# Gated linear attention inside a two-block layer: chunks of 128 tokens in place of 64, decays measured from the middle of a chunk, masks as bits, and the two directions' scores added by GpSimd

## The chip, the core and the metric

One core of a Trainium2 chip runs one program, which holds the two blocks of a layer. Times are device microseconds (us) of that core, as the median of several runs; lower is better. The engines are TensorE (PE; its weight loads are listed apart as PEld), VectorE (DVE), ScalarE (ACT), GpSimd (POOL) and SyncE (SP), which issues most of the transfers.

## The reference

The first block (attention, a gated delta rule, a gated mix) is not touched. The second block normalises its input, mixes tokens with a gated linear attention in both directions plus an average pooling, and ends with a mixture of 32 experts. The part that matters is the linear attention over 512 tokens, with 4 heads of 64 key and 128 value features, and with start states that a scan over 256 context tokens gives:

```
b = cumsum(la, within a chunk)                   # la: log of the decay, <= 0
k_st = k * exp(b_last - b)
d_state = k_st^T v                               # one 64x128 matrix a chunk and head
S_next = exp(b_last) * S + d_state               # scan over the chunks
qb, kb = q * exp(b), k * exp(-b)
scores = where(mask, qb kb^T, 0)
o = scores v + qb S_prev
out = o_f + flip(o_b)                            # both directions added
```

The reference uses CHUNK = 64. Its result does not depend on the chunk length but for rounding.

## The kernel before

Everything stays in one large SBUF tile, `arena`, whose parts are handed on from stage to stage. Every engine runs one list of instructions, written by hand, and waits on named semaphores. `bank("s")` and `bank("v")` give TensorE the next of four PSUM banks of two rings, `pss` (read by ScalarE, mostly) and `psv` (read by VectorE, mostly). `L.did` makes an engine wait for its own instruction; `L.need` waits for another engine's.

The linear attention lies at 1071 to 1142 us of the trace, in three parts.

1. Decays (1071 to 1092 us). For the four pairs of direction `d` and pair of heads `m2`, `decay_sums` sums the log decays of each tile of 128 tokens by a product with a triangle of ones that is cut at 64 tokens (`blk`). ScalarE makes `eb`, `enb` (exp of plus and minus the sum) and `dec2` (exp at the chunk's last token); VectorE multiplies them into `qb` and `kb` (`decayed`). `decay_rests` gives the sums from a token to its chunk's end; ScalarE and VectorE turn them into the keys `kst`. The pooling's products (`pool`) lie between.
2. Scan (1092 to 1117 us). Twelve steps `n`: four chunks of the context, then eight of the sequence. A step issues `kst^T v` of 64 tokens for both directions (line 1401); VectorE adds them to the decayed state (line 3174) and keeps the state ahead of each sequence chunk in `sprev`. In steps 0, 2, 4 and 6 lie the scores of one pair (line 1412), which VectorE multiplies with the mask (lines 3186, recorded as the helper's line 2621). Other products are put between: `pool_out` (line 1352), `gate_row` (line 1377), and, ahead of step 9, a product with the router's weights (recorded as L884), whose result ScalarE copies to `lshift`.
3. Outputs (1117 to 1142 us). For each `m2` two banks collect `scm v` of both directions (line 1426, 32 products of 128 columns in all) and `sprev^T qb` per chunk (line 1430, 64 products of 64 columns, with the two heads in the two halves of the array's rows).

After that ScalarE squares and copies the four results (lines 2271, 2272), TensorE sums the squares (line 1457), and the output projection and the router follow. The weights of the output projection's last part, `wo23`, are loaded into the place where `sprev` lay, so SyncE issues that load (line 1670) when the outputs' products are done, and line 1457 waits for it. Behind it SyncE issues the first loads of the experts' weights.

## Time and profile before

| | |
|---|---|
| median of 3 runs | 1481.84 us (1479.63 to 1483.26) |
| the profiled execution | 1489.19 us, of which the profile's span is 1487.4 us |
| TensorE busy | 1400.6 us, 94% of the span |
| VectorE busy | 723.8 us, 49% |
| ScalarE busy | 382.0 us, 26% |
| GpSimd busy | 421.5 us, 28% |
| mean granted clock of TensorE | 0.972 of full speed |

Busy shares are means over stages with different limits; what counts for the change is which wait ends last in the linear attention's own 70 us.

### The profile page before, as it was taken

The page shows a single profiled execution, that of the slowest core. Times are in us where ns is not written, and L with a number is a line of the kernel's source. Part 1 is how long each engine was busy: PE and PEld are TensorE (multiplying, and loading weights), DVE is VectorE, ACT ScalarE, POOL GpSimd, SP SyncE. Part 2 cuts the span into 40 slices and gives each one's busy share as a digit, 9 for nine tenths or more (in the row PEclk, how much of TensorE's full clock was granted, in tenths as well). Part 3 has the DMA queues.
Part 4 walks back from the last instruction along what each step waited for, and adds up shares of the span by engine and source line. Part 5 has one row for each costly group of instructions (what it writes and reads, how often), then busy time and mean ns, then how long its engine had stood idle before and what let it go on. Part 6 is the DMA issues. An engine that isn't in the chain of part 4 may idle for free. (4 is left out here: it accounts for less than half of the span.)

```text
span 1487.4 us, 22182 instructions
## 1 busy us (share of the span) xinstructions
PE 1400.6 (94%) x8580; PEld 966.8 (65%) x8580; DVE 723.8 (49%) x1284; ACT 382.0 (26%) x773; POOL 421.5 (28%) x316
## 2 busy tenths in 40 slices
PE   6998999999999989999999999999998979998876
PEld 4865556885554458778888868878867864333222
DVE  5261572124449988778624252731471454332325
ACT  2313564104343233332110022511531011000002
POOL 3410020620005526654545535045000003111110
PEclk9999999999999999999999999999996988999999
DMA  8227210113112113314232311241302858999996
GB/s 318 88 86 285 83 58 29 71 71 113 57 58 85 57 58 147 141 59 187 111 134 96 142 57 57 65 124 57 121 26 108 345 207 309 416 419 419 422 417 258
DMA packets 48439, 236.51 MB, mean 159 GB/s; under 512 B 12135, under 2 KB 13423, under 8 KB 27600
## 3 DMA queue, kind: packets, MB, share of 16 engines
q1 hardware_dynamic: 42720, 224.48, 38.8%
q0 software_dynamic: 5040, 8.27, 1.5%
q10 hardware_dynamic: 576, 2.36, 0.4%
q8 instruction: 69, 1.13, 0.3%
q14 instruction: 34, 0.28, 0.1%
HBM read 223.66 MB, written 21.51 MB: 165 GB/s over the span
## 5 line engine op out<-in xcount | busy, mean ns | idle before, releaser
L922 PE MATMUL psv<-arena 128*128 128x256 f32 x1648 | 362.8, 380 | 1.9 <-DVE arena L2691 1.9
L922 PEld LDWEIGHTS psv<-arena 128*128 128x128 f32 x1648 | 314.1, 191 | 46.0 <-issue 3.2
L2624 DVE TENSOR_TENSOR arena<-arena,psv 128x512 f32<-128x512 f32 (+1 forms) x99 | 68.6, 693 | 275.4 <-PE psv L922 273.4
L884 PE MATMUL psv<-arena,wslot 128*128 128x512 f32 x384 | 170.7, 598 | 0.0
L1542 PE MATMUL pss<-arena 128*64 128x512 f32 x432 | 122.2, 636 | 14.7 <-DMA arena<-w_expert_in 13.6
L884 PEld LDWEIGHTS psv<-arena,wslot 128*128 128x128 f32 x384 | 71.2, 190 | 83.2 <-issue 82.9
L884 PE MATMUL pss<-arena 128*128 128x512 f32 (+1 forms) x256 | 106.2, 568 | 1.4 <-ACT arena L2019 1.4
L2854 DVE SCALAR_TENSOR_TENSOR arena<-psv,ccols,arena 128x510 f32<-128x510 f32 (+1 forms) x96 | 71.9, 749 | 50.0 <-ACT arena L2075 46.7
L922 PE MATMUL psv<-arena,wslot 128*128 128x256 f32 x384 | 86.3, 380 | 2.3 <-DVE arena L2624 1.3
L1885 ACT ACTIVATE arena<-pss 128x512 f32<-128x512 f32 (+2 forms) x89 | 51.5, 579 | 129.0 <-PE pss L884 64.3
L1542 PEld LDWEIGHTS pss<-arena 128*64 128x64 f32 x432 | 38.3, 145 | 69.8 <-issue 69.7
L884 PEld LDWEIGHTS pss<-arena 128*128 128x128 f32 x256 | 47.7, 190 | 51.6 <-issue 48.4
L922 PEld LDWEIGHTS psv<-arena,wslot 128*128 128x128 f32 x384 | 72.6, 190 | 13.2 <-issue 2.3
L922 PE MATMUL psv<-wslot,arena 128*128 128x256 f32 x320 | 72.6, 381 | 6.2 <-ACT arena L1944 2.7
L2408 POOL TENSOR_TENSOR arena<-wslot 128x1024 f32<-128x1024 f32 x11 | 26.4, 2396 | 176.5 <-PE pss L1064 90.4
L2426 POOL TENSOR_TENSOR arena<-arena 128x1024 f32<-128x1024 f32 x20 | 49.1, 2453 | 81.0 <-DVE arena L2717 35.8
L922 PEld LDWEIGHTS psv<-wslot,arena 128*128 128x128 f32 x320 | 60.3, 190 | 16.0 <-ACT arena L1944 3.9
L3328 DVE TENSOR_TENSOR arena<-pss,arena 128x256 f32<-128x256 f32 x16 | 6.8, 425 | 128.7 <-ACTq L233 128.7
L2621 DVE TENSOR_TENSOR arena<-arena 128x512 f32<-128x512 f32 (+2 forms) x64 | 51.4, 803 | 32.6 <-ACT arena L2031 22.3
L1561 PE MATMUL psv<-arena 128*64 128x512 f32 x236 | 54.8, 598 | 3.0 <-ACTq L233 1.6
L2624 DVE TENSOR_TENSOR arena<-arena 128x512 f32<-128x512 f32 (+4 forms) x67 | 53.4, 797 | 3.0
L2295 ACT ACTIVATE arena<-pss 128x256 f32<-128x256 f32 x16 | 6.2, 384 | 184.0 <-PE pss L1542 184.0
(411 smaller groups left out, 2066.7 us busy)
## 6 DMA issues: line engine op xcount, KB each, us to landing
wslot<-w_blocks SPq DMA_DIRECT2D x56, 1024.0 KB, 5.2
arena<-w_blocks SPq DMA_DIRECT2D x30, 1024.0 KB, 6.3
arena<-w_expert_out SPq DMA_DIRECT2D x29, 1024.0 KB, 25.0
arena<-w_expert_in SPq DMA_DIRECT2D x28, 1024.0 KB, 26.7
arena<-w_expert_in SPq DMA_DIRECT2D x28, 512.0 KB, 7.9
arena<-w_expert_in SPq DMA_DIRECT2D x6, 2048.0 KB, 25.7
y_dram<-arow SPq DMA_DIRECT2D x1, 4096.0 KB
arena<-c_pool SPq DMA_DIRECT2D x4, 1024.0 KB, 8.8
```

What stands on the lines that cost most here:

```text
L884: m = mm(o, l, r, start=(n == 0), stop=(n == len(pairs) - 1))
L922: m = mm(o[:, j * HALF_T:(j + 1) * HALF_T], l[:, c, j * P:(j + 1) * P], r[:, c, :], start=new and j == 0 and c == 0, stop=j == 1 and c == ...
L1542: m = mm(o[x * CAP:(x + 1) * CAP, :], xe[:, k, c, x * CAP:(x + 1) * CAP], win[2 * w + x][:, c, :], start=(c == 0), stop=(c == KC - 1))
L1561: m = mm(o[x * CAP:(x + 1) * CAP, :], hidT[:, k, c, x * CAP:(x + 1) * CAP], wout_home(n, x, c)[:, c0:c0 + 512], start=(c == 0), stop=(c == 1))
L1885: L.did(A(dst, src, func, **kw), s[sig] if sig else None, [s["free_s"]])
L2295: L.did(A(sil[:, k, :], pss[:, (q0 + job) % 4, 0:DE], ACT.Silu), None, [s["sil_ready"]])
L2408: L.did(TT(part[0], a21, a22, ALU.add), s["part_ready"])
L2426: L.did(TT(term[n], lo, hi, ALU.subtract), s["term_ready"])
L2621: L.did(V.tensor_tensor(o, x, y, ALU.mult), *sig)
L2624: L.did(V.tensor_tensor(o, x, y, ALU.add), *sig)
L2854: L.did(V.scalar_tensor_tensor(o[:, lo:hi], b[:, lo + m:hi + m], tap(j, k), o[:, lo:hi], ALU.mult, ALU.add), s["conv_ready"] if k == 4 els ...
L3328: L.did(V.tensor_tensor(hid[:, k, :], pss[:, (s0 + job) % 4, DE:2 * DE], sil[:, k, :], ALU.mult), s["hid_ready"], [s["free_s"], s["sil_use ...
```

## The change

Chunks are 128 tokens, one tile, so the scan has two context steps and three sequence steps whose state is needed on (`LAST_STATE` = 5), and each step contracts 128 tokens.

The sums that go into `eb` and `enb` are now taken from the middle of the tile: the constants `sums_of` hold the triangle less the column of the first (or last) half, and two further columns that give the tile's whole sum and the sum up to its middle. So the product has 130 columns for a sequence tile and 2 for a context tile, and `dec2` holds both decays. A state is needed as seen from the middle too: ScalarE multiplies each `sprev` by the decay up to the middle, 16 instructions of 128x128 into the half of `sprev` that is now free.

The scores of a pair lie in each of the steps 0 to 3. Their mask is no product with 0 or 1 any more, but a bitwise AND of the scores' bits with a mask of integers, `kept`, that VectorE makes once (two instructions). GpSimd adds the scores of the two directions, four instructions of 128x512, so line 1426's products are half as many.

```diff
@@ -82,10 +85,14 @@
-    c[:, C_BLE:C_BLE + P] = same & (p <= f)
-    c[:, C_BGE:C_BGE + P] = same & (p >= f)
-    c[:, C_BGT:C_BGT + P] = same & (p > f)
-    c[:, C_BLT:C_BLT + P] = same & (p < f)
+    c[:, C_BLE:C_BLE + P] = p <= f
+    c[:, C_BGE:C_BGE + P] = p >= f
+    c[:, C_BGT:C_BGT + P] = p > f
+    for d, (sums, half) in enumerate(((p <= f, p < CH2), (p >= f, p >= CH2))):
+        o = C_SUMS + d * GSUM
+        c[:, o:o + P] = sums.astype(np.float32) - half
+        c[:, o + P:o + P + 1] = 1.0
+        c[:, o + P + 1:o + P + 2] = half
...
@@ -279,8 +286,10 @@
-        blk = [const[:, C_BLE:C_BLE + P], const[:, C_BGE:C_BGE + P]]
-        blk_rest = [const[:, C_BGT:C_BGT + P], const[:, C_BLT:C_BLT + P]]
+        kept_both = ctx.enter_context(nc.sbuf_tensor("kept", [P, 2, P], I32))
+        kept = [kept_both[:, d, :] for d in range(2)]
+        sums_of = [const[:, C_SUMS + d * GSUM:C_SUMS + (d + 1) * GSUM] for d in range(2)]
+        rest_of = [const[:, C_BGT:C_BGT + P], const[:, C_LT:C_LT + P]]
...
@@ -792,25 +801,20 @@
             r = P // GRID_W
             return max(0, r * t - below) * GRID_W, min(SEQ // GRID_W, r * t + r + above) * GRID_W
-        def chunk_at(d, n):
-            c = n if n < 4 else n - 4
-            if d:
-                c = (3 if n < 4 else 7) - c
-            return (NT if n < 4 else 0) + c // 2, c % 2
-        def chunk_col(d, n):
-            t, u = chunk_at(d, n)
-            return 2 * t + u
+        def tile_at(d, n):
+            if n < NTC:
+                return NT + (NTC - 1 - n if d else n)
+            return NT + NTC - 1 - n if d else n - NTC
         def state_at(d, m2, n):
-            if n < 4:
+            if n < NTC:
                 return swork[:, n % 2, d, m2, :]
-            if n == 12:
-                return None
-            t, u = chunk_at(d, n)
-            return sprev[:, d, m2, 2 * t + u, :]
+            return sprev[:, d, m2, tile_at(d, n), :]
+        LAST_STATE = NT + NTC - 1
+        DELTA_STATES = 4 * (NCK - 1)
         def scale_rows(eng, L, V, g):
@@ -1324,16 +1328,19 @@
             def decay_sums(n):
                 d, m2 = divmod(n, 2)
                 col = d * 256 + m2 * P
-                for t0, many in ((0, NT), (NT, NTC)):
-                    o = bank("s")
-                    for t in range(many):
-                        m = mm(o[:, t * P:(t + 1) * P], la[:, t0 + t, col:col + P], blk[d], start=True, stop=True)
+                for tiles in (range(NT - 1), range(NT - 1, NT + NTC)):
+                    o, at_ = bank("s"), 0
+                    for t in tiles:
+                        r = sums_of[d] if t < NT else sums_of[d][:, P:]
+                        n_ = GSUM if t < NT else 2
+                        m = mm(o[:, at_:at_ + n_], la[:, t, col:col + P], r, start=True, stop=True)
+                        at_ += n_
                     m.then_inc(s["full_s"], 1)
             def decay_rests(t):
                 o = bank("s")
                 for d in range(2):
-                    m = mm(o[:, d * 256:(d + 1) * 256], blk_rest[d], la[:, t, d * 256:(d + 1) * 256],
+                    m = mm(o[:, d * 256:(d + 1) * 256], rest_of[d], la[:, t, d * 256:(d + 1) * 256],
                            start=True, stop=True)
                 m.then_inc(s["full_s"], 1)
@@ -1379,31 +1386,29 @@
                 m.then_inc(s["full_s"], 1)
             L.need(s["k2_ready"])
-            for n in range(12):
-                if n in (0, 4, 6):
+            for n in range(LAST_STATE):
+                if n in (0, 2, 3):
                     L.need(s["kst_ready"], 2)
-                for g in {0: (0, 1), 1: (2,), 2: (3,)}.get(n, ()):
+                for g in {0: (0, 1), 1: (2, 3)}.get(n, ()):
                     pool_out(g)
-                if n in (3, 5):
-                    gate_row(0 if n == 3 else 4)
-                if n == 9:
+                if n in (2, 3):
+                    gate_row(0 if n == 2 else 4)
+                if n == 4:
                     pe.wait_ge(s["ld_wrt"], 32)
                     o = bank("s")
                     product(o[:, 0:NG + NE], [(mod[:, 24 + c, 0:1].broadcast_to([P, P]), wrt[:, c, :])
                                               for c in range(KC)]).then_inc(s["full_s"], 1)
                 for d in range(2):
-                    t, u = chunk_at(d, n)
+                    t = tile_at(d, n)
                     o = bank("v")
-                    tok = slice(u * CH2, (u + 1) * CH2)
                     for m2 in range(2):
                         for hh in range(2):
                             h = 2 * m2 + hh
-                            m = mm(o[HX[hh], m2 * P:(m2 + 1) * P], kst[tok, t, d * 256 + h * 64:d * 256 + (h + 1) * 64],
-                                   v2[tok, t, h * P:(h + 1) * P], start=True, stop=True)
+                            m = mm(o[HX[hh], m2 * P:(m2 + 1) * P], kst[:, t, d * 256 + h * 64:d * 256 + (h + 1) * 64],
+                                   v2[:, t, h * P:(h + 1) * P], start=True, stop=True)
                     m.then_inc(s["full_v"], 1)
-                if n % 2 == 0 and n < 2 * H2:
-                    m2, d = divmod(n // 2, 2)
+                if n < 2 * 2:
+                    m2, d = divmod(n, 2)
                     if n == 0:
                         L.need(s["qb_ready"], 4)
                     o = [bank("v"), bank("v")]
@@ -1414,21 +1419,22 @@
                     for hh in range(2):
                         m[hh].then_inc(s["full_v"], 1)
-            L.need(s["sc_ready"], 2 * H2)
-            L.need(s["sprev_ready"])
             for m2 in range(2):
+                L.need(s["scm_ready"], 2)
                 o = [bank("s"), bank("s")]
+                for hh in range(2):
+                    h = 2 * m2 + hh
+                    for t in range(NT):
+                        tk = slice(t * P, (t + 1) * P)
+                        mm(o[hh][:, tk], v2[:, t, h * P:(h + 1) * P], scm[2 * h][:, tk],
+                           start=t == 0, stop=False, skip_group_check=True)
+                if m2 == 0:
+                    L.need(s["sprev_ready"], 2 * 2 * NT)
                 for d in range(2):
-                    for hh in range(2):
-                        h = 2 * m2 + hh
-                        for t in range(NT):
-                            tk = slice(t * P, (t + 1) * P)
-                            mm(o[hh][:, tk], v2[:, t, h * P:(h + 1) * P], scm[2 * h + d][:, tk],
-                               start=(d == 0 and t == 0), stop=False, skip_group_check=True)
-                    for c in range(8):
-                        ck = slice(c * CH2, (c + 1) * CH2)
-                        m = [mm(o[hh][:, ck], sprev[HX[hh], d, m2, c, :], qb[HX[hh], d, m2, ck], start=False,
-                                stop=(d == 1 and c == 7), skip_group_check=True) for hh in range(2)]
+                    for t in range(NT):
+                        tk = slice(t * P, (t + 1) * P)
+                        m = [mm(o[hh][:, tk], sprev[HX[hh], d, m2, NT + t, :], qb[HX[hh], d, m2, tk], start=False,
+                                stop=(d == 1 and t == NT - 1), skip_group_check=True) for hh in range(2)]
                 for hh in range(2):
                     m[hh].then_inc(s["full_s"], 1)
             products_by["attention", 0] = jobs["s"]
@@ -2249,13 +2255,19 @@
                 b = full()
                 if n >= 2:
                     act.wait_ge(s["qb_ready"], n - 1)
-                L.did(A(eb[:, n % 2, :], b, ACT.Exp, scale=1.0 / GATE_NORM))
-                L.did(A(enb[:, n % 2, :], b, ACT.Exp, scale=-1.0 / GATE_NORM))
-                ends = b.rearrange("p (c i) -> p c i", i=CH2)[:, :, CH2 - 1 if d == 0 else 0]
-                L.did(A(dec2[:, d, m2, 0:8], ends, ACT.Exp, scale=1.0 / GATE_NORM), s["bexp_ready"], [s["free_s"]])
+                b = b[:, 0:(NT - 1) * GSUM].rearrange("p (t i) -> p t i", i=GSUM)
+                most = slice(0, (NT - 1) * P)
+                L.did(A(eb[:, n % 2, most].rearrange("p (t i) -> p t i", i=P), b[:, :, 0:P], ACT.Exp,
+                        scale=1.0 / GATE_NORM))
+                L.did(A(enb[:, n % 2, most].rearrange("p (t i) -> p t i", i=P), b[:, :, 0:P], ACT.Exp,
+                        scale=-1.0 / GATE_NORM))
+                L.did(A(dec2[:, d, m2, 0:NT - 1, :], b[:, :, P:GSUM], ACT.Exp, scale=1.0 / GATE_NORM), s["bexp_ready"],
+                      [s["free_s"]])
                 b = full()
-                ends = b[:, 0:CTX].rearrange("p (c i) -> p c i", i=CH2)[:, :, CH2 - 1 if d == 0 else 0]
-                L.did(A(dec2[:, d, m2, 8:12], ends, ACT.Exp, scale=1.0 / GATE_NORM), s["bexp_ready"], [s["free_s"]])
+                L.did(A(eb[:, n % 2, (NT - 1) * P:], b[:, 0:P], ACT.Exp, scale=1.0 / GATE_NORM))
+                L.did(A(enb[:, n % 2, (NT - 1) * P:], b[:, 0:P], ACT.Exp, scale=-1.0 / GATE_NORM))
+                L.did(A(dec2[:, d, m2, NT - 1:, :].rearrange("p t k -> p (t k)"), b[:, P:P + 2 * (1 + NTC)], ACT.Exp,
+                        scale=1.0 / GATE_NORM), s["bexp_ready"], [s["free_s"]])
             for t in STATES:
                 evict(kst[:, t, :], 512, "kexp_ready", ACT.Exp, scale=1.0 / GATE_NORM)
             L.did(A(ss[:, 60:61], eps, ACT.Sqrt))
@@ -2265,6 +2277,13 @@
             for c0 in (0, 512):
                 evict(gtrow[:, c0:c0 + 512], 512, None)
             evict(lshift, NG + NE, None)
+            for n in range(NTC, NT + NTC):
+                for d in range(2):
+                    t = tile_at(d, n)
+                    act.wait_ge(s["st_ready"], DELTA_STATES + 2 * (n - NTC) + d + 1)
+                    for m2 in range(2):
+                        L.did(A(sprev[:, d, m2, NT + t, :], sprev[:, d, m2, t, :], ACT.Copy,
+                                scale=dec2[:, d, m2, t, 1:2]), s["sprev_ready"])
             L.need(s["qb_ready"], 4)
             for h in range(H2):
                 b = full()
@@ -2519,6 +2538,10 @@
+            for m2 in range(2):
+                L.need(s["sc_ready"], 4)
+                for h in (2 * m2, 2 * m2 + 1):
+                    L.did(TT(scm[2 * h], scm[2 * h], scm[2 * h + 1], ALU.add), s["scm_ready"])
...
@@ -3149,6 +3172,8 @@
+            for d, c in enumerate((C_BLE, C_BGE)):
+                L.did(V.tensor_scalar(kept[d], const[:, c:c + P], -1.0, None, ALU.mult))
...
@@ -3164,27 +3189,21 @@
             pooled(3)
             L.did(V.memset(swork[:, 0, :, :, :], 0.0))
-            for n in range(12):
+            assert L.raised[s["st_ready"]] == DELTA_STATES, L.raised[s["st_ready"]]
+            for n in range(LAST_STATE):
                 for d in range(2):
                     b = full()
-                    c = chunk_col(d, n)
-                    if n == 11:
-                        L.raise_(s["free_v"])
-                        continue
-                    ins = [V.scalar_tensor_tensor(state_at(d, m2, n + 1), state_at(d, m2, n), dec2[:, d, m2, c:c + 1],
+                    t = tile_at(d, n)
+                    ins = [V.scalar_tensor_tensor(state_at(d, m2, n + 1), state_at(d, m2, n), dec2[:, d, m2, t, 0:1],
                                                   b[:, m2 * P:(m2 + 1) * P], ALU.mult, ALU.add) for m2 in range(2)]
                     L.go(ins[0])
-                    if d:
-                        L.did(ins[1], s["free_v"])
-                    else:
-                        L.go(ins[1], s["free_v"])
-                if n % 2 == 0 and n < 2 * H2:
-                    m2, d = divmod(n // 2, 2)
+                    L.did(ins[1], s["st_ready"] if n + 1 >= NTC else None, [s["free_v"]])
+                if n < 2 * 2:
+                    m2, d = divmod(n, 2)
                     for hh in range(2):
                         b = full()
-                        mul(by4(scm[2 * (2 * m2 + hh) + d]), by4(b), over(blk[d], 4), s["sc_ready"], [s["free_v"]])
-            L.raise_(s["sprev_ready"])
+                        L.did(V.tensor_tensor(by4(scm[2 * (2 * m2 + hh) + d].bitcast(I32)), by4(b.bitcast(I32)),
+                                              over(kept[d], 4), ALU.bitwise_and), s["sc_ready"], [s["free_v"]])
             for h in range(H2):
                 L.need(s["rt2_ready"])
                 o = catT[:, h, :]
```

Two places show how the instructions stand now. TensorE, from the last score products through the scan's end and the outputs (`pss` and `psv` are the two rings of banks, `wrt` the router's weights). Before:

```order
L1401 MATMUL psv<-arena 64x128 x16
L1412 MATMUL psv<-arena 128x128 x8
L1401 MATMUL psv<-arena 64x128 x16
L884 MATMUL pss<-wrt,mod 128x36 x8
L1401 MATMUL psv<-arena 64x128 x24
L1426 MATMUL pss<-arena 128x128 x8
L1430 MATMUL pss<-arena 128x64 x16
```

And now, where L1384 is `gate_row`, L1407 the scan's product, L1417 the scores, L888 the router's product, L1429 and L1436 the outputs:

```order
L1384 MATMUL pss<-const,mod 128x128 x4
L1407 MATMUL psv<-arena 64x128 x8
L1417 MATMUL psv<-arena 128x128 x8
L888 MATMUL pss<-wrt,mod 128x36 x8
L1407 MATMUL psv<-arena 64x128 x8
L1429 MATMUL pss<-arena 128x128 x8
L1436 MATMUL pss<-arena 128x128 x16
L1429 MATMUL pss<-arena 128x128 x8
L1436 MATMUL pss<-arena 128x128 x16
```

Behind the router's product stand 8 products of the scan instead of 24, and the outputs are 48 products, all of 128 columns, instead of 96.

ScalarE, from the pooling's results to the outputs' squares. Before (L2264 scales the pooling's results, L1885 copies `gtrow` and then `lshift`, L2271 and L2272 square and copy a head's output):

```order
L2264 ACTIVATE arena<-pss,cols 128x512 x4
L1885 ACTIVATE gtrow<-pss 128x512 x2
L1885 ACTIVATE arena<-pss 128x36
L2271 ACTIVATE arena<-pss 128x512
L2272 ACTIVATE arena<-pss 128x512
```

And now:

```order
L2276 ACTIVATE arena<-pss,cols 128x512 x4
L1891 ACTIVATE gtrow<-pss 128x512 x2
L1891 ACTIVATE arena<-pss 128x36
L2285 ACTIVATE arena<-arena 128x128 x16
L2290 ACTIVATE arena<-pss 128x512
L2291 ACTIVATE arena<-pss 128x512
```

All 16 scalings of the states (L2285) stand behind the copy of `lshift`, which waits for the router's product.

## Rows read from the trace of the kernel before

**Rows 1.** The page: granted clock of TensorE in 40 slices of 37 us, tenths.

```profile
PEclk9999999999999999999999999999996988999999
```

**Rows 2.** Windows: length, busy of PE, PEld, DVE, ACT, POOL, then clock, DMA share, GB/s.

```profile
1094.00:1117.00 23.00, 21.08 (x293) 16.32 (x292) 18.02 (x53) 3.68 (x7) 0.00 (x0) 0.91 0.00 1
1117.00:1142.00 25.00, 24.75 (x192) 23.55 (x192) 1.50 (x2) 2.40 (x5) 0.00 (x0) 0.61 0.00 1
1142.00:1147.00 5.00, 0.01 (x1) 0.04 (x3) 1.50 (x2) 2.38 (x4) 0.00 (x0) 0.65 0.81 308
```

**Rows 3.** Windows again, shorter ones around the clock's changes, and one of the experts.

```profile
1105.00:1112.00 7.00, 5.90 (x95) 4.79 (x94) 6.12 (x17) 0.60 (x1) 0.00 (x0) 1.00 0.00 0
...
1117.00:1130.00 13.00, 12.79 (x82) 12.26 (x82) 0.00 (x0) 0.00 (x0) 0.00 (x0) 0.50 0.00 0
1130.00:1136.00 6.00, 6.00 (x38) 5.66 (x38) 1.50 (x2) 2.39 (x4) 0.00 (x0) 0.50 0.01 3
1137.00:1142.00 5.00, 4.96 (x68) 4.64 (x66) 0.00 (x0) 0.01 (x1) 0.00 (x0) 1.00 0.00 0
...
1300.00:1400.00 100.00, 86.89 (x398) 33.13 (x396) 31.81 (x77) 5.38 (x14) 17.02 (x29) 0.95 1.02 420
```

**Rows 4.** Timeline of PE in the scan; two records are one product.

```profile
1092.40 1.88 PE L1352 MATMUL pss<-arena 128*128 128x512 f32 x4
1094.21 0.68 PE L1401 MATMUL psv<-arena 64*64 64x128 f32 x16
1094.82 1.16 PE L1412 MATMUL psv<-arena 64*128 64x128 f32 x16
...
1100.34 1.16 PE L1377 MATMUL pss<-const,mod 128*128 128x128 f32 x8
...
1111.16 2.21 PE L884 MATMUL pss<-wrt,mod 128*128 128x36 f32 x16
1113.30 3.53 PE L1401 MATMUL psv<-arena 64*64 64x128 f32 x48
```

**Rows 5.** Timeline of PE in the outputs and at the stage behind them.

```profile
1120.89 3.68 PE L1430 MATMUL pss<-arena 64*128 64x64 f32 x32
1124.50 3.78 PE L1426 MATMUL pss<-arena 128*128 128x128 f32 x16
...
1137.98 2.05 PE L1426 MATMUL pss<-arena 128*128 128x128 f32 x16
1139.96 2.00 PE L1430 MATMUL pss<-arena 64*128 64x64 f32 x32
1146.99 1.94 PE L1457 MATMUL pss<-arena,const 128*32 128x512 f32 x8 [5.03 <-DMA arena<-w_blocks]
```

**Rows 6.** Timeline of SP's queue at the outputs' end.

```profile
1142.03 0.34 SPq L1670 DMA_DIRECT2D arena<-w_blocks  x1
```

**Rows 7.** Timelines of ACT and PE in the decays.

```profile
1081.08 0.60 ACT L2252 ACTIVATE arena<-pss 128x512 f32<-128x512 f32 x1 [0.55 <-DVE arena L2621]
...
1082.95 2.77 ACT L1885 ACTIVATE arena<-pss 128x512 f32<-128x512 f32 x4
...
1082.62 1.99 PE L1336 MATMUL pss<-arena,const 128*128 128x256 f32 x8 [0.29 <-ACTq L233]
```

**Rows 8.** Timeline of DVE at the end of the decays and in the scan.

```profile
1092.67 0.69 DVE L3145 COPY arena<-psv 128x512 f32<-128x512 f32 x1 [2.11 <-PE psv L1345]
...
1094.99 1.12 DVE L3174 SCALAR_TENSOR_TENSOR arena<-arena,psv 128x128 f32<-128x128 f32 x4 [0.86 <-PE psv L1401]
1096.15 1.53 DVE L2621 TENSOR_TENSOR arena<-psv,const 128x512 f32<-128x512 f32 x2
```

**Rows 9.** Timeline of PE elsewhere: products of the form 128x64 by 128 columns.

```profile
523.82 1.09 PE L968 MATMUL pss<-const,arena 128*64 128x128 f32 x16
```

**Rows 10.** Groups by form, whole trace: busy, mean ns | idle before.

```profile
L1971 ACT ACTIVATE arena<-arena 128x128 f32<-128x128 f32 x40 | 11.9, 297 | 21.2 <-DVE arena L2624 21.1
...
L1914 ACT ACTIVATE arena<-pss,gain 128x128 f32<-128x128 f32 x16 | 5.9, 368 | 25.1 <-PE pss L960 24.7
...
L2384 POOL TENSOR_TENSOR arena<-arena 128x512 f32<-128x512 f32 x16 | 18.5, 1158 | 7.9 <-ACTq L1920 5.4 <-ACT arena L1885 1.6
```

More of the change, by code:

```diff
@@ L10 @@
 U32 = mybir.dt.uint32
+I32 = mybir.dt.int32
 ALU = mybir.AluOpType
@@ L56 @@
 C_BLE = C_DG + CK
-C_BGE, C_BGT, C_BLT = C_BLE + P, C_BLE + 2 * P, C_BLE + 3 * P
-C_IOTA = C_BLE + 4 * P
+C_BGE, C_BGT = C_BLE + P, C_BLE + 2 * P
+C_SUMS = C_BLE + 3 * P
+GSUM = P + 2
+C_IOTA = C_SUMS + 2 * GSUM
 C_TOK = C_IOTA + CAP
@@ L457, in build @@
         enb = at(top[0], 2, SEQ)
-        dec2 = at(top[0], 2, 2, 12)
+        dec2 = at(top[0], 2, 2, NT + NTC, 2)
         swork = at(top[0], 2, 2, 2, P)
```

2 lines of the change are left out of this document (1 added, 1 removed).

## The prediction

> **What bounds the kernel now.** I looked first for where TensorE loses time. The page's row of granted clocks has one dent in the middle of the run, in two slices around 1120 us [rows 1], and the linear attention lies there. Its windows show two stretches. In the scan (1094 to 1117 us) TensorE is busy 21.1 of 23 us and VectorE 18.0, in short pieces that wait for one another. In the outputs (1117 to 1142 us) TensorE is busy 24.75 of 25 us, nobody else has work, and its mean clock is 0.61 [rows 2]. The shorter windows say why 0.61: the clock is full up to 1112 us, at half (1.2 of 2.4 GHz) from 1117 to 1136 us though the engine is never idle, and full again from 1137 us [rows 3]. So eight products of 128 columns take 3.78 us at half clock and 2.05 at full, and sixteen of 64 columns 3.68 and 2.00 [rows 5]. TensorE sets the end of this stage, mostly at half clock.
>
> What hangs on that end? SyncE issues the load of `wo23` at 1142.03 us, as the outputs end [rows 6], and TensorE sits 5.03 us until it has landed [rows 5]. The transfer engines move nothing before it: 0.00 of their time in the scan and in the outputs [rows 2]. The experts' weights come behind this load on the same queue, at 420 GB/s with a DMA share of 1.02 later on [rows 3]. A stage bound by transfers would swallow a gain only if its transfers were already under way; here they start after the outputs. If the outputs end X earlier, the load, the projection, the router and the experts all start X earlier. So the working is that of one moment: the outputs' end, 1141.96 us now (1139.96 plus 2.00) [rows 5].
>
> **The change, step by step, at full clock unless said.**
>
> *Decays.* ScalarE has six instructions a pair instead of four: two of 384 columns, two of 128 and two tiny ones, for two of 512 and two tiny. A pair takes 1.87 us now (1081.08 to 1082.95) [rows 7]; the two of 384 save some 0.2, the two of 128 cost about 0.3 each [rows 10], so about 0.4 more. That is 1.6 us on ScalarE for four pairs, part of it in time in which it waits for VectorE. TensorE's `decay_rests` wait for the banks that ScalarE frees (0.29 us now) [rows 7], so I add 0.45 us to TensorE's path. VectorE comes about 1 us later, hidden by its 2.11 us of waiting for the last pooling product [rows 8]; without that cover it would be 1 us. `decay_sums` has as many products as before, narrow ones among them; I cost it at nothing, and the cover is the same wait. The two instructions that make `kept` fall into a pause of VectorE earlier on. The scan starts at 1092.40 + 0.45 = 1092.85 us [rows 4].
>
> *Scan.* Twelve pairs of 64-token products become five of 128 tokens. A pair costs 0.61 us now (1094.21 to 1094.82) [rows 4]. The new form, 128x64 weights and 128 columns with two heads side by side, occurs elsewhere: eight products in 1.09 us [rows 9], about 1.05 without the last one's drain. So 5 x 1.05 = 5.25. The rest stays: four `pool_out` 3.6 (two take 1.8, 1092.40 to 1094.21), four scores 4 x 1.1, two `gate_row` 2 x 1.1, the router's product 2.2 [rows 4]. Sum 17.65, so the router's product ends at 1109.45 us and the last scan product at 1110.5. VectorE is no bound: a step is four updates (1.12) and two masks (1.53) [rows 8], 2.8 us with the gaps, while TensorE needs 3.25 and more for each of steps 1 to 3. This takes the AND for as fast as the product that it replaces; no row has it, and the bounds are the 1.53 us of two products and, above, the rival below. The first half of the score-by-`v` products, now eight, needs GpSimd's sums of the first two heads. Their masks are done at about 1102.6, and GpSimd's sum of this size takes 1.16 us [rows 10], so they are there at about 1105, and those of the other two heads at about 1112. Both are early: hidden by the scan, and worth 2.3 us in the worst case if that were gone. The eight products add 2.0 us: 1112.5 us.
>
> *A new wait.* Next TensorE needs all 16 scaled states, and these stand on ScalarE behind the copy of `lshift`, hence behind the router's product. They could begin with the first sequence state; they begin at 1109.75 us. One costs between 0.30 us (SBUF to SBUF, no scale taken from memory) and 0.37 (from PSUM, with such a scale) [rows 10]. Both properties meet here, and each waits for its predecessor, so I take 0.42 a piece with the gap, bounds 0.33 and 0.45: 6.7 us, until 1116.5. TensorE sits 4.0 us, and queued behind are all the remaining outputs, for which ScalarE's squares and the load wait. So by this point most of what the shorter scan gave is used up: 1116.5 against the 1117.2 at which the outputs began (1113.30 plus 3.53, and a short pause) [rows 4], but with the first eight products already done.
>
> *Outputs.* Left are 16 state products, 8 of scores, 16 of states. State products with 128 columns have the form of the scores (eight in 1.1 us at full clock) [rows 4]: 2.2 a group, and 2.0 for the eight of 128 rows. At full clock 6.4 us, end 1122.9. At half clock the eight take 3.75, and sixteen state products between 3.68 (their old form of half the columns) and 4.4 (twice 2.2) [rows 5]; with 4.2 that is 12.1 us, end 1128.6. The clock: before, it fell in the scan, and the pause of 4 us is a second occasion, as it is low in the pause from 1142 to 1147, too (mean 0.65) [rows 2]. But the products of 64 columns, under which it stayed low for 19 us, are gone, and it came back during a group of the dense ones. The rows do not decide between the ends, so I take the middle, 1125.7 us.
>
> The sum: 1141.96 - 1125.7 = 16.3 us. Against it, the constants have 132 columns more, 67 KB, 0.2 us at the 420 GB/s of [rows 3] if the start waits for all of it. Net 16.1 us. The profiled execution took 1489.19 us (span 1487.4), 7.3 us above the median of the runs, so it would become 1473.1, and the median 1481.84 - 16.1 = 1465.7 us.
>
> **A page against the trace.** The rows show TensorE busy without a break from 1117 to 1136 us at 0.50 of its clock [rows 3]. The Trainium skill (TensorE: Matmul & The Clock Gate, "What's actually happening") says that the throttled clock is the default and that the engine's activity releases it. By that rule the dense outputs would run at full clock nearly from their start, and the sum would be 19 us in place of 16; the trace agrees only in part, since 19 us of unbroken work did not release it.
>
> **The rivals.**
>
> *Full clock in the outputs.* The work after the pause is all of the dense kind that brought the clock back. End at 1122.9, gain 18.9, time 1462.9 us. Against it: the pause just ahead.
>
> *Half clock to the end.* The clock stays low over the whole 12.1 us, as it did over 19. End at 1128.6, gain 13.2, time 1468.6 us.
>
> *A dearer wait.* ScalarE's copies cost 0.6 us each (a form not in the trace, and a semaphore to wait for each time): 9.6 us, until 1119.4, 2.9 us later than in my sum, and with the low clock behind it the end is at 1131, gain 10 to 11, time about 1471 us.
>
> *The experts swallow it.* If the transfers of the experts' weights were bound by something that does not move with the outputs, the time would stay at 1481.8. For it: a DMA share of 1.02 in that stage [rows 3]. Against it: no transfer runs before 1142 us [rows 2].
>
> *Slower.* VectorE's AND on 32-bit integers out of PSUM is slow. The trace has no such row; the product that it replaces takes 0.76 us. To eat the 16 us and VectorE's spare time in the scan (about 0.5 us in each of four steps), eight of them would have to cost 18 us more, 2.3 each; from 3.1 us an AND on, the kernel is slower. With 4 us an AND it would be 8 x 3.3 - 2 - 16, about 8 us slower: 1490 us. I see no reason for it.
>
> **How the numbers follow.** A measurement here tells about 0.3%, 4.4 us, from no change. Chances: my forecast, a clock that is mixed (1463.5 to 1468), 0.45; full clock 0.15; half clock 0.17; dearer wait or another loss in part 0.12; swallowed 0.07; slower 0.04. Faster: the first four, 0.89; same 0.07; slower 0.04. The range holds the first three and most of the fourth: from 1460 (full clock, and copies at 0.33 us) to 1473 (dearer wait and half clock). The predicted time is 1465.7 us.
>
> **What the profile would show.** Right: the AND at about 0.7 us; the router's product ending near 1109.5; the copies of the states starting only behind `lshift` and ending near 1116.5, with TensorE idle for about 4 us until then; the outputs ending between 1123 and 1129; and from `wo23`'s load on the same rows, 16 us earlier. Wrong: a DVE wait between scores and scan products; states that are ready before TensorE asks; GpSimd's sums asked for before they are there; or a distance from the load of `wo23` to the end that is not that of before. The prediction is most exposed to TensorE's clock, in the outputs and in the first products behind the load, and to the price of ScalarE's copies.

## The result, and the profile after

The changed kernel takes 1473.97 us (median of five, 1471.97 to 1475.90) where the kernel before takes 1481.84 (1479.63 to 1483.27) on the same chip. The ratio is 0.9941 with an interval of 0.9923 to 0.9959: 7.9 us or 0.59% faster. I had predicted 1465.7 us, with a range up to 1473. The sign is right and the size is half of what I said (16.1 us).

The profiled execution of the changed kernel took 1475.9 us (span 1473.9). First its page: busy times, then TensorE's granted clock in 40 slices of 37 us, to be held against [rows 1].

```profile
PE 1387.6 (94%) x8372; PEld 952.7 (65%) x8372; DVE 717.0 (49%) x1262; ACT 389.6 (26%) x797; POOL 426.2 (29%) x320
...
PEclk9999999999999999999999999999998989999989
```

The slice of the dent (the 31st, 1115 to 1153 us before) is an 8 now and was a 6. (It is one slice, not two, as I had it; the two 8s behind it in [rows 1] lie at 1190 to 1264 us, behind the linear attention.) The timeline of PE in the scan and the outputs, which answers to [rows 4, 5]:

```profile
1095.03 1.88 PE L1359 MATMUL pss<-arena 128*128 128x512 f32 x4
1096.84 1.09 PE L1407 MATMUL psv<-arena 128*64 128x128 f32 x16
1097.87 1.16 PE L1417 MATMUL psv<-arena 64*128 64x128 f32 x16
...
1109.39 1.97 PE L888 MATMUL pss<-wrt,mod 128*128 128x36 f32 x16
1111.30 1.09 PE L1407 MATMUL psv<-arena 128*64 128x128 f32 x16
1112.32 2.05 PE L1429 MATMUL pss<-arena 128*128 128x128 f32 x16
1118.69 3.55 PE L1436 MATMUL pss<-arena 64*128 64x128 f32 x32 [4.32 <-ACT arena L2285]
1122.17 2.15 PE L1429 MATMUL pss<-arena 128*128 128x128 f32 x16
1124.25 2.06 PE L1436 MATMUL pss<-arena 64*128 64x128 f32 x32
1131.42 1.94 PE L1463 MATMUL pss<-arena,const 128*32 128x512 f32 x8 [5.11 <-DMA arena<-w_blocks]
```

The windows of the same kernel (length, busy of PE, PEld, DVE, ACT, POOL, clock, DMA share, GB/s):

```profile
1096.00:1118.00 22.00, 18.37 (x199) 14.56 (x197) 12.08 (x29) 9.96 (x22) 5.08 (x4) 1.00 0.00 1
1118.00:1127.00 9.00, 7.61 (x80) 7.08 (x80) 1.50 (x2) 3.63 (x8) 0.00 (x0) 0.81 0.01 2
```

The predicted wait stands where it was predicted: TensorE waits 4.32 us for ScalarE's L2285, the copies of the scaled states. Ahead of it the clock is full, through the whole scan. Behind it the granted clock is at half (0.50) from 1119 to 1122 us, so the first group of state products takes 3.55 us where the last one, at full clock, takes 2.06; the next group is nearly all at full clock (2.15 us for 2.05). Now the other engines. ACT and POOL by their timelines, then two groups of the lines by form:

```profile
1111.41 0.20 ACT L1891 ACTIVATE arena<-pss 128x36 f32<-128x36 f32 x1 [3.42 <-PE pss L888]
1111.73 6.91 ACT L2285 ACTIVATE arena<-arena 128x128 f32<-128x128 f32 x16
```
```profile
1104.70 2.62 POOL L2544 TENSOR_TENSOR arena<-arena 128x512 f32<-128x512 f32 x2 [61.66 <-DVE arena L3205]
1111.17 2.62 POOL L2544 TENSOR_TENSOR arena<-arena 128x512 f32<-128x512 f32 x2 [3.85 <-DVE arena L3205]
```
```profile
L2285 ACT ACTIVATE arena<-arena 128x128 f32<-128x128 f32 x16 | 6.4, 401 | 0.6
...
L3205 DVE TENSOR_TENSOR arena<-psv,kept 128x512 int32<-128x512 int32 x8 | 5.5, 692 | 1.2 <-PE psv L1417 0.5
```

The sixteen copies run one straight after the other behind the router's copy, 6.91 us in all, 0.43 us each. The bitwise mask costs 0.69 us. GpSimd's sums are ready at 1107.3 and 1113.8 us, before TensorE asks for them (1112.3 and 1122.2). SyncE issues the load of `wo23` again as the outputs end (1126.31 us), where it stood at 1142.03 us in [rows 6]:

```profile
1126.37 0.34 SPq L1676 DMA_DIRECT2D arena<-w_blocks  x1
```

**Where the difference to the profile of before comes from.** I mark one stretch in each trace: L, from the first `pool_out` product (the start of the scan) to the end of the outputs. Before it was 1092.40 to 1141.96, 49.56 us; after it is 1095.03 to 1126.31, 31.28 us. My prediction had 1092.85 to 1125.7, 32.85 us. So this stretch became 18.3 us shorter where I said 16.7 (16.3 net of the 0.45 us ahead of it). The spans, though, differ by 13.5 us only (1487.4 to 1473.9): the rest of the program is 4.8 us longer (1442.6 for 1437.8): 2.6 us ahead of the marked stretch (1095.03 for 1092.40), of which 0.45 were predicted, and 2.2 behind it. And the medians differ by 7.9 us. So the mechanism is all there, and yet half the gain is missing against the median. Two theories:

A. The stretch of low clock in the outputs of before has no fixed length. The profiled execution of before, 7.3 us above its median, had a long one; a typical execution has a shorter one, and there is less to gain than I took from it.

B. The gain is the same in every execution, and some 8 us of it are lost elsewhere: in the experts, or in the start with its larger constants.

If A holds, L of before varies, and the rest does not differ between the two kernels. If B holds, the rest is longer in the changed kernel.

### The profile page after: what moved, and what is told of

It is laid out like the page before. It is cut to its first block, busy times and chain, and to the rows that moved or that the text cites. A ratio compares the mean times of both kernels' runs of the same rounds, so it can differ in the third digit from the quotient of the medians.

```text
span 1473.9 us, 21769 instructions
## 1 busy us (share of the span) xinstructions
PE 1387.6 (94%) x8372; PEld 952.7 (65%) x8372; DVE 717.0 (49%) x1262; ACT 389.6 (26%) x797; POOL 426.2 (29%) x320
## 4 chain that ended last, share of the span: by engine, by line
PE 77%; DVE 10%; DMA 5%; SPq 3%; ACT 2%; issue 2%; DVEq 0%; POOL 0%; ACTq 0%; POOLq 0%
PE psv L926 33%; PE psv L888 14%; PE pss L888 7%; PE pss L1548 5%; DMA arena<-w_expert_in 4%; PE psv L1567 2%; DVE arena L2647 2%; SPq L1694 2%; PE pss L1068 1%; DVE arena L2967 1%; PE pss L972 1%; PE pss L989 1%; DVE arena L2644 1%; DVE arena L2932 1%; PE psv L964 1%
## 5 line engine op out<-in xcount | busy, mean ns | idle before, releaser
L888 PE MATMUL psv<-arena,wslot 128*128 128x512 f32 x384 | 170.7, 598 | 0.0
L888 PEld LDWEIGHTS psv<-arena,wslot 128*128 128x128 f32 x384 | 71.2, 190 | 83.2 <-issue 82.9
L888 PE MATMUL pss<-arena 128*128 128x512 f32 (+1 forms) x256 | 106.2, 568 | 1.4 <-ACT arena L2025 1.4
L926 PE MATMUL psv<-wslot,arena 128*128 128x256 f32 x320 | 75.6, 392 | 6.2 <-ACT arena L1950 2.7
L888 PEld LDWEIGHTS pss<-arena 128*128 128x128 f32 x256 | 47.7, 190 | 51.6 <-issue 48.4
```

Of the source, the lines that this page charges most:

```text
L888: m = mm(o, l, r, start=(n == 0), stop=(n == len(pairs) - 1))
L926: m = mm(o[:, j * HALF_T:(j + 1) * HALF_T], l[:, c, j * P:(j + 1) * P], r[:, c, :], start=new and j == 0 and c == 0, stop=j == 1 and c == ...
```

## The experiments

Below, "its chip's before" is the kernel before as timed beside the run on the same chip. Ratios are to it, with 95% intervals. before_a, before_b, after_a and early ran on one chip, the other runs on another.

**The kernel before, thrice more (before_a, before_b, before_c), and the changed one again (after_a).** No edit.

> The kernel before, unchanged, profiled once more. My prediction took the outputs' 24.8 us and the clock of 0.61 in them from one profiled execution of 1489.2 us, 7.3 us above the median. Theory A (the profiled execution is not typical: the clock stays low in the outputs for a length that differs from one execution to the next): a median near 1482, and in this profile the outputs take another time than 24.8 us, from about 14 (full clock) to 25 us, with the whole time moving by the same amount. Theory B (the local gain is the 16 to 18 us that the two profiles show in every execution, and the changed kernel loses 8 us elsewhere): the outputs take 24 to 25 us again, and this execution too lies near 1482 to 1489 us.

> The kernel before a further time, one look. By theory A the outputs' length differs from the other two profiles of this kernel, anywhere from 14 to 25 us; by theory B it is 24 to 25 us for the third time.

> The changed kernel, unchanged, profiled once more, on the same chip as the kernel before. Both theories: 0.994 of the kernel before, 8 us. Theory A: the stretch from the first output product to the last (13.99 us in the first profile, of which 4.3 us a wait for the states) differs by up to 4 us by the clock. Theory B: the stages outside the linear attention are 5 to 8 us longer than those of the kernel before in both profiles.

> One more look at the kernel before. Its outputs have taken 24.8, 17.3 and 21.4 us in three profiles, with the clock low for 23.8, 9 and 20 us from its fall on. If the length of the low stretch differs freely from one execution to the next, this look gives a fourth value between 16 and 25 us; most executions (1477 to 1482 us of span) should look like the shortest.

Times: before_a 1484.32 us, ratio 1.0015 (0.9989 to 1.0041); after_a 1472.08, ratio 0.9928 (0.9901 to 0.9955). That is a gain of 9.8 us against its chip's before (1481.88) and of 12.2 against before_a, the same kernel on the same chip. The profile of before_a (span 1480.3), timeline of PE in the outputs and one window:

```profile
1118.32 3.65 PE L1426 MATMUL pss<-arena 128*128 128x128 f32 x16 [0.37 <-issue]
1121.89 2.00 PE L1430 MATMUL pss<-arena 64*128 64x64 f32 x32
...
1133.63 2.00 PE L1430 MATMUL pss<-arena 64*128 64x64 f32 x32
1140.66 1.93 PE L1457 MATMUL pss<-arena,const 128*32 128x512 f32 x8 [5.03 <-DMA arena<-w_blocks]
```
```profile
1118.00:1136.00 18.00, 17.32 (x192) 16.52 (x192) 1.50 (x2) 2.72 (x5) 0.00 (x0) 0.90 0.00 1
```

The same instructions in the same order, but only the first group of the outputs is slow; the clock is back at 1122 us, where it came back between 1136 and 1137 us before [rows 3]. In before_b (span 1490.4) it came back during the fourth group:

```profile
1119.88 3.75 PE L1426 MATMUL pss<-arena 128*128 128x128 f32 x16 [0.38 <-issue]
...
1130.89 2.58 PE L1430 MATMUL pss<-arena 64*128 64x64 f32 x32
```

and in before_c (span 1488.9) during the sixth, as in the first profile:

```profile
1117.35 3.75 PE L1426 MATMUL pss<-arena 128*128 128x128 f32 x16 [0.38 <-issue]
...
1135.67 2.54 PE L1430 MATMUL pss<-arena 64*128 64x64 f32 x32
1138.14 2.05 PE L1426 MATMUL pss<-arena 128*128 128x128 f32 x16
```

Put side by side, with L and the rest of the span (microseconds):

| profile | span | L | rest |
|---|---|---|---|
| before, the one predicted from | 1487.4 | 49.6 | 1437.8 |
| before_a | 1480.3 | 41.7 | 1438.6 |
| before_b | 1490.4 | 46.4 | 1444.0 |
| before_c | 1488.9 | 49.6 | 1439.3 |
| after | 1473.9 | 31.3 | 1442.6 |
| after_a | 1470.3 | 31.2 | 1439.1 |

L of before spreads over 8 us, and that of the changed kernel does not move, though up to 4 us of movement had been allowed for it. The rest is 1438 to 1444 us, and its spread is common to both kernels: its mean is 1439.5 us over the six profiles of this study with a scan of 64 tokens, and 1440.1 over the seven with 128 tokens. So B's 5 to 8 us are not there. That speaks for A and against B. The unprofiled executions say which length is typical: in most of each chip's before, the span is 1477 to 1483 us with a mean clock of 0.975 to 0.979, as in before_a; in some (4 of 18 on this chip, 7 of 25 on the other one) it is 1484 to 1494 us. That 41.7 us is the typical L rests on this span and on one profile. With it the gain in L is 10.4 to 10.5 us, less 0.5 for the longer decays ahead of it, and the runs show 7.9 to 12.2 by medians (the interval of the first, 0.9923 to 0.9959, is itself 6 to 11 us). One expectation missed: before_c was to look like the typical ones most likely, and showed the long stretch again. Three of the four profiles had a stretch longer than the typical; why profiled executions should, or whether three of four is chance, stays open.

**ScalarE's copies as soon as their states are there (early).** The same instructions; only the place of the copies in ScalarE's program changes.

```diff
-            for c0 in (0, 512):
-                evict(gtrow[:, c0:c0 + 512], 512, None)
-            evict(lshift, NG + NE, None)
-            for n in range(NTC, NT + NTC):
+            def middle_states(n):
...
+            evict(gtrow[:, 0:512], 512, None)
+            middle_states(NTC)
+            evict(gtrow[:, 512:1024], 512, None)
+            middle_states(NTC + 1)
+            middle_states(NTC + 2)
+            evict(lshift, NG + NE, None)
+            middle_states(NTC + 3)
```

> ScalarE scales the states of the first three sequence steps between its other copies, ahead of the router's product, and only the last step's four behind it. If the wait of 4.3 us is owed to their place in ScalarE's list, the last state is ready 0.5 to 1 us after TensorE asks, so 3.5 us are saved, and up to 3 us more if the pause was what kept the clock low behind it: 0.2 to 0.45% faster than the changed kernel, 1467.5 to 1470.5 us. If the wait was only a part of a bound that something else sets (VectorE's last update), TensorE waits for that and nothing is saved.

1465.05 us (1463.71 to 1468.71), ratio 0.9885 (0.9851 to 0.9919), against 0.9928 of the changed kernel beside it: 7.0 us less. It is also faster than expected (1467.5 to 1470.5 us), because no wait at all is left where 0.5 to 1 us was expected. ACT and PE of its timeline:

```profile
1105.41 3.44 ACT L2282 ACTIVATE arena<-arena 128x128 f32<-128x128 f32 x8
1108.89 0.20 ACT L1891 ACTIVATE arena<-pss 128x36 f32<-128x36 f32 x1
1109.62 1.70 ACT L2282 ACTIVATE arena<-arena 128x128 f32<-128x128 f32 x4 [0.53 <-DVE arena L3202]
```
```profile
1109.30 2.05 PE L1429 MATMUL pss<-arena 128*128 128x128 f32 x16
1111.37 2.06 PE L1436 MATMUL pss<-arena 64*128 64x128 f32 x32
1113.36 2.05 PE L1429 MATMUL pss<-arena 128*128 128x128 f32 x16
1115.34 2.06 PE L1436 MATMUL pss<-arena 64*128 64x128 f32 x32
1122.44 1.88 PE L1463 MATMUL pss<-arena,const 128*32 128x512 f32 x8 [5.05 <-DMA arena<-w_blocks]
```

The wait is gone, and the low clock with it. L is 25.40 us for 31.18. Of these 5.8 us, 4.3 are the wait and 1.5 the clock (3.55 less 2.06). The last microsecond of the 7.0 is within the intervals. Taken once more (early_b, below), this version took 1467.59 us, with the same L and the clock full again. It beats both kernels.

**Both groups of score products ahead of the wait (swap).** TensorE works on while ScalarE copies.

```diff
+            both = []
             for m2 in range(2):
                 L.need(s["scm_ready"], 2)
                 o = [bank("s"), bank("s")]
+                both.append(o)
...
-                if m2 == 0:
-                    L.need(s["sprev_ready"], 2 * 2 * NT)
+            L.need(s["sprev_ready"], 2 * 2 * NT)
+            for m2 in range(2):
+                o = both[m2]
```

> The changed kernel with TensorE's second group of score products ahead of its wait for the scaled states, where the first stands; ScalarE's order is not touched. The group takes 2.0 us and falls into the wait, which shrinks from 4.3 to 2.3 us: 2 us faster than the changed kernel. If the low clock of the first state products (3.55 us for what takes 2.06) comes from the pause, a pause of 2.3 us makes it rarer, up to 1.5 us more: 1468.5 to 1470.5 us. If only ScalarE's order mattered, no change.

1469.99 us (1467.92 to 1472.58), ratio 0.9908 (0.9878 to 0.9939). Timeline of PE, and a window over the state products:

```profile
1110.59 3.84 PE L1431 MATMUL pss<-arena 128*128 128x128 f32 x32
1116.96 5.27 PE L1439 MATMUL pss<-arena 64*128 64x128 f32 x64 [2.53 <-ACT arena L2288]
```
```profile
1116.90:1122.30 5.40, 5.27 (x64) 5.08 (x64) 0.48 (x1) 1.60 (x4) 0.00 (x0) 0.71 0.01 3
```

The wait shrinks by 1.8 us, the length of the second group, to 2.53, and L to 28.9. The clock (mean 0.71) is low behind the shorter pause too, for a part of 5.27 us where full clock takes 4.1. So what is left of the wait costs about 3.7 us (2.5 of waiting and 1.2 of clock), as the step to early (another 3.5 in L) confirms.

**The sums of both directions undone in the changed kernel (no_add), the same in early (early_no_add), and done alone in the kernel before (before_add).** The score products go back to one set for each direction, or, in the kernel before, become one set with GpSimd's sums ahead. The edit of no_add; that of before_add is its reverse:

```diff
-                L.need(s["scm_ready"], 2)
+                L.need(s["sc_ready"], 4)
...
+                for d in range(2):
...
-                        mm(o[hh][:, tk], v2[:, t, h * P:(h + 1) * P], scm[2 * h][:, tk],
-                           start=t == 0, stop=False, skip_group_check=True)
+                            mm(o[hh][:, tk], v2[:, t, h * P:(h + 1) * P], scm[2 * h + d][:, tk],
+                               start=(d == 0 and t == 0), stop=False, skip_group_check=True)
...
-            for m2 in range(2):
-                L.need(s["sc_ready"], 4)
-                for h in (2 * m2, 2 * m2 + 1):
-                    L.did(TT(scm[2 * h], scm[2 * h], scm[2 * h + 1], ALU.add), s["scm_ready"])
```

> The changed kernel without GpSimd's sums: TensorE runs all 32 score products again, everything else as changed. Two groups of eight come back, 2.0 us each at full clock. The first falls into the wait of 4.3 us for the scaled states and should cost nothing; the second lies on the path. So 2 us slower than the changed kernel (1474 to 1476 us) if the wait is a wait as read, 4 us slower if it is not. With the pause down to 2.3 us the clock may stay up, which would give 1 to 2 us back.

> The kernel before with one part of the change: GpSimd adds the two directions' scores and TensorE runs 16 score products instead of 32; chunks of 64 tokens, masks by product, everything else as before. The products left out cost 2.0 us for eight at full clock. If the part is worth what its products cost, the outputs become 4.0 us shorter at equal clock (16 at full clock becomes 12) and the run about 0.27% faster. If the outputs were set by the clock rather than by the work, less dense work keeps the clock low for longer and part of the 4 us is lost: 0 to 0.15%.

no_add: 1475.01 us (1471.18 to 1481.61), ratio 0.9949 (0.9929 to 0.9969), 1 to 3 us above the changed kernel's two medians, neither of which was timed beside it. L is 31.48, 0.2 to 0.3 more than with the sums, though TensorE has 3.6 us more of products to do. Timeline of PE:

```profile
1111.39 3.84 PE L1430 MATMUL pss<-arena 128*128 128x128 f32 x32
1117.77 2.06 PE L1437 MATMUL pss<-arena 64*128 64x128 f32 x32 [2.53 <-ACT arena L2286]
1119.75 3.84 PE L1430 MATMUL pss<-arena 128*128 128x128 f32 x32
```

Eight products of the sixteen lie in the wait (2.53 for 4.32), and here the clock came out full behind it, which saves 1.5 us: 3.6 - 1.8 in the wait - 1.5 is the 0.3 of L. So in the changed kernel GpSimd's sums gained little in L; by the medians, whose intervals overlap, 1 to 3 us. before_add: 1478.55 us (1473.42 to 1484.56), ratio 0.9965 (0.9940 to 0.9989), 3.7 us less than its chip's before (1482.29), where the sixteen products left out are worth 4.0 at full clock.

> The kernel with the scaled states moved ahead in ScalarE's list, once more. Its first profile showed no pause at all and full clock in the outputs (8.1 us from first to last product). If both belong together, the second profile shows the same, and the median lies at 1464 to 1467 us. If the clock was luck, this profile has a low stretch in the outputs and the executions spread like those of the changed kernel.

> The same without GpSimd's sums: TensorE runs all 32 score products. In the changed kernel leaving the sums out cost 1 to 3 us only, as the first group's 2.0 us fell into the wait for the states. If that wait is why the sums give less than their 4 us, they give the whole 4 us here, where there is no wait: outputs of 12 us at full clock in place of 8.1, and 1468.5 to 1470.5 us. If the sums are worth less for another reason (GpSimd takes 1.31 us each, VectorE's updates are 0.06 us longer in the changed kernel), it is again 1 to 3 us.

early_b 1467.59 us, ratio 0.9897 (0.9868 to 0.9925); early_no_add 1472.28, ratio 0.9927 (0.9899 to 0.9954). Both lie above the times expected of them (by 0.6 and 1.8 us); the difference is near the 4 us expected. Between them lie 4.7 us of medians and 3.5 us of L (25.39 and 28.88). With the wait gone the sums are worth what their two groups of eight products take, 1.79 us each, 3.6 in all: a part of the change that pays in full only when another part is mended.

**The router's product earlier (router_early).** In the kernel before, the clock's first slow rows stand at the router's product or just behind it [rows 4]. It has 36 columns; if it tips the clock, moving it moves the fall.

```diff
-                if n == 9:
+                if n == 5:
```

> The kernel before with the router's product at step 5 of the scan instead of step 9, same instructions otherwise. It has 36 columns a product, so it streams little, and in all three profiles of the kernel before the clock fell during it or right behind it. If that product, next to the short products of 64 tokens, is what tips the clock, then with it elsewhere the clock stays full to the outputs or falls at the new place and is back by then: outputs near 16 us, median 1 to 2 us lower, and none of the executions near 1490 us. If the short products alone do it, the clock falls as before and the spread stays (about one execution in four 8 to 12 us above the rest).

1481.92 us (1478.97 to 1490.34), ratio 0.9999 (0.9976 to 1.0021). Timeline of PE:

```profile
1106.74 1.87 PE L884 MATMUL pss<-wrt,mod 128*128 128x36 f32 x16
1108.54 1.18 PE L1401 MATMUL psv<-arena 64*64 64x128 f32 x32
1110.51 2.03 PE L1412 MATMUL psv<-arena 64*128 64x128 f32 x16 [0.79 <-DVE arena L3174]
1112.47 6.40 PE L1401 MATMUL psv<-arena 64*64 64x128 f32 x80
1119.25 3.75 PE L1426 MATMUL pss<-arena 128*128 128x128 f32 x16 [0.38 <-issue]
```

The router's product and the products after it run at full clock, and the fall comes at about 1110.5 us, in the scan's own products (2.03 us for a group of scores that took 1.16). So it is not the router's product. By windows of 1 us the clock is back at 1114 us and falls a second time at about 1117.3, still under the scan's products, and it is low until 1124 us. The spread stays as well: one of the ten executions took 1490.34 us. Over all profiles of this study the clock fell inside the scan in the six that have a scan of 64 tokens (before four times, before_add, router_early) and in none of the seven with 128 tokens. How long it stays low then varies: L is 43.7 in router_early and 37.4 in before_add.

## Why the prediction was off

*What bounds the kernel, and that all follows the outputs' end.* Right. The outputs' end and the load of `wo23` moved together, and the rest of the span is 1437.6 to 1444.0 us in all thirteen profiles, however early the outputs ended, while L goes from 49.6 to 25.4. The load of `wo23` keeps TensorE waiting 5.0 to 5.2 us in each, and the experts move with it. "Swallowed by the experts" is refuted.

*Decays.* Right. From TensorE's first product with the sums to the first `pool_out` it takes 21.87 us (1073.16 to 1095.03) for 21.35 before (1071.05 to 1092.40): 0.5 us for my 0.45, and the same in every profile of either kind within 0.02. ScalarE's pair takes 2.26 us (1083.88 to 1086.14) for my 2.3. VectorE's later end is hidden: its wait behind it is 1.74 us for 2.11.

*Scan.* Right. From the first `pool_out` to the last scan product it takes 17.3 us (1095.03 to 1112.3) for my 17.65. Most of the difference is the router's product: 1.91 us (1109.39 to 1111.30) for my 2.2, a price taken from a row in which the clock was already falling (0.88 of full from 1112 to 1113 us). A step's eight products take 1.03 us up to the next group for my 1.05, and the bitwise AND 0.69 us, the price of the product it replaces; the rival "slower" falls with it. VectorE's four updates take 1.36 us for the 1.12 that I took over, hidden too. GpSimd's sum takes 1.27 us for my 1.16 and is hidden, as said.

*The new wait.* Right: 4.32 us for 4.0, a copy at 0.43 us for 0.42, begun behind `lshift`. "Dearer wait" is refuted. And early shows that the wait is the price of an order, not of the arithmetic.

*Outputs.* The middle between the clock's levels was right in kind: behind the wait one group in four is at half clock, 1.5 us in all. From the wait's end to the outputs' end 7.6 us pass (1118.69 to 1126.31), 9.2 by my sum. L is 31.2 to 31.3 us for the predicted 32.85. One reading behind this term was wrong: I wrote that the clock came back "during a group of the dense ones". It came back between 1136 and 1137 us, in the group of 64-column products that starts at 1135.53 (2.52 us; the dense group before it took 3.78 throughout):

```profile
1131.82 3.78 PE L1426 MATMUL pss<-arena 128*128 128x128 f32 x16
1135.53 2.52 PE L1430 MATMUL pss<-arena 64*128 64x64 f32 x32
```

It came back within 64-column products in before_b, before_c and router_early too. So the argument that these products kept the clock low and the dense ones brought it back, in the forecast and in the rival of full clock, had no support in the rows.

*The step that failed is the last, the subtraction.* The working up to the outputs' end erred by 1.6 us in L, and to the other side. What failed is this: "The profiled execution took 1489.19 us, 7.3 us above the median of the runs, so it would become 1473.1, and the median 1465.7." A gain worked out on one execution was taken off the median, as if the 7.3 us lay elsewhere. They lay in the very stretch that the change removes: its 19 us of half clock in the outputs. before_a, at the span of a typical execution, has 3.4 us of it there, and its L is 7.9 us shorter and its span 7.1. The 1141.96 in "1141.96 - 1125.7 = 16.3 us" belongs to a long execution. With the typical L of 41.7 my own terms would have given 41.7 - 32.85 - 0.45 (decays) - 0.2 (constants) = 8.2 us, hence 1473.6 us, where 1473.97 was measured. That this agrees so closely is in part luck: with the measured L of 31.2 the same working gives 9.8 and 1472.0 us, which is still within the interval of the result. I had both facts in front of me, the 7.3 us and the 0.61, and didn't ask whether one was the other. The first profile of the changed kernel, at 1475.9 us, fits the 1473.1 that I gave for the profiled execution within 2.8 us, but L was 1.6 us shorter than I said and the rest of the span 4.8 us longer, of which 0.65 were predicted; the other 4 lie within the spread of the rest. Both profiles lie above their kernels' medians, so this one comparison hid the fault.

*The page against the trace.* The Trainium skill (TensorE: Matmul & The Clock Gate, "What's actually happening") has the engine's activity release the throttled clock. In before_a the clock was back after one group of the outputs' products, in before_c after five and a half, all unbroken: the traces agree that the clock ends full under busy work, and show that this can take 3.4 us of the outputs (before_a) or 19.4 (before_c).

**What stays open.** What in the 64-token scan tips the clock was not isolated. The scan with 128 tokens has fewer and wider products, and it has none of the pauses of 0.65 us in which TensorE waits for VectorE, and no run changed one without the other. Nor is it known what decides between a short and a long low stretch. Behind a pause of TensorE the clock was low in two of two profiles with 4.32 us, in one of two with 2.53, and full in three of three without one; that is few.

## What to carry to other kernels

When the profiled execution stands several microseconds off the median, find where these lie before a gain worked out on it is taken off the median: if they lie in the stretch that the change touches, they are part of the supposed gain. A stretch at a low clock is the first suspect. Profile the same kernel several times, and hold the span and the mean clock of each profile against those of the timed executions, to see which length is usual: one more profile need not show it, as before_c repeated the long stretch of the first. And where a shortened stage runs into a new wait, look at what is queued ahead of the late work on the engine that does it: sixteen copies that stood behind one eviction of 36 columns cost 5.8 us in L and 7.0 in the median, and hid what another part of the change was worth.

## What the runs showed of the hardware

The granted clock of TensorE can fall without a long pause ahead of it. In the kernel before, TensorE was busy for 5.90 of the 7 us up to 1112 us [rows 3], with no pause over 0.65 us, and the clock fell at about 1112.8. How long it stays low differs between executions of the same program: by windows of 1 us about 24 us in the first profile (1113 to 1137), 7 in before_a (1115 to 1122), 17 in before_b (1115 to 1132) and 24 in before_c (1113 to 1137), where the expectation of before_c had put 9 and 20 for before_a and before_b. In the window of before_b that lies in it, TensorE is busy for all of 11 us:

```profile
1120.00:1131.00 11.00, 11.00 (x66) 10.44 (x66) 0.00 (x0) 0.00 (x0) 0.00 (x0) 0.50 0.00 0
```

A bitwise AND on 32-bit integers out of PSUM, 128x512, costs VectorE 0.69 us, no more than the fp32 product in its place.
